# Modulation tiles beside the mixers: one PSUM bank, shifted condition columns, one turn per stage

## The chip, the cores and the metric

The kernel runs on one core of a Trainium2 chip. The metric is the device time of one execution in microseconds (us). Before the change three runs took 3722.24, 3710.8 and 3716.47 us, median 3716.47.

## The reference

Two blocks of a small transformer are computed one after the other on 256 tokens of 1024 features, both with two layers. What matters here is the modulation: a vector of conditions times a large weight matrix gives shifts, scales and gates for all tokens.

```
cond = silu(c)
for l in range(2):
    mod = cond @ w_ada[l] + b_ada[l]              # 1024 x 6144
    sh1, sc1, gt1, sh2, sc2, gt2 = split(mod, 6)
    proj = (x * (1 + sc1) + sh1) @ w_in[l]
    ... hgrn2_chunkwise and stick_breaking_attention (the mixers) ...
    ... merge, w_o, layer norm, PEER experts ...
second block, per layer i:
    mx = silu(c_2)   @ w_mod_2[i] + b_mod_2[i]    # 1024 x 9216
    mz = silu(c_ctx) @ w_mod_2[i] + b_mod_2[i]
```

## The kernel before

All large weights stream from memory in tiles of 1024 x 512 (2 MB), each as two halves of 1 MB, into `raw`, which has room for four halves. The SyncE queue issues the loads in order (`WeightStream.load`, L218); a load into a slot waits until TensorE has used the half that lay there, four halves earlier. Groups of tiles follow each other in a fixed list: `ada0`, `in0`, `beside0`, `gates0` and so on, and the first two tiles of a group are loaded while the group before it is being used. Groups with `split` are first rounded by ScalarE (`split_hi`, L263) and subtracted by VectorE (`split_lo`, L276); the modulation tiles are used as they land.

A modulation tile costs eight products. `cond` holds for each of the eight chunks of 128 features a block of 32 columns, of which the first three are the conditions and the others zero. `strip_products` (L777) multiplies chunk k into the 32 PSUM partitions from 32*(k%4), so four strips hold partial sums of the same rows. The strips are added and the row is turned into columns by four more matmuls, which take the row as the stationary operand and a 0/1 matrix `strip_sum` as the moving one.

The change is about the mixer stage of each layer (`mixers`), which is one block: all engines start it together and the next block starts when the last is through. Its own work is a chain of eight levels across the engines: VectorE makes exponents (L1301, L1303), ScalarE takes the exponential (L1265), VectorE multiplies (L1315, L1316), TensorE makes scores (L1222; L1234 at the last level), VectorE keeps them (L1288). Between these runs `StickBreaking`, one group of heads per two levels: scores (L1116), four ScalarE activations (`logs`, L1144 to L1147), VectorE (`losses`, L1157 to L1161), sums on TensorE (L1124 to L1126), VectorE (`rest`, L1166 to L1169), ScalarE (L1151), values on TensorE (L1134, L1136), and VectorE (`keep`, L1174, L1175), which the next group's scores wait for. After the levels come the outputs (L1244, L1247), their norm on VectorE (L1341 to L1351), eight transposes (L1256) and VectorE's last work (L1362, L1364), then `split_lo` for the first tile of the gates.

Beside it `SideModulation` does 12 modulation tiles in layer 0 and 10 in layer 1. `halves` puts two halves (one tile) behind each level on TensorE, and what is left behind the outputs: three tiles in layer 0, one in layer 1. Tiles alternate between two PSUM banks. `turn_row` (L1721) of tile t-1 stands between the two halves of tile t, and ScalarE's `copies` has for each tile a copy of the row out of PSUM (L1760), for which it waits until the tile's products are made, and a copy of the turned columns (L1748). A tile's first product waits until the columns two tiles back are copied. The engines execute their instructions in order, so each of these waits holds what is queued behind it. At the end VectorE adds the biases in two instructions (L1370) ahead of `split_lo`.

`input_projection` is the block ahead of the mixers. There VectorE first clears three tiles (L1031) and then waits for the first rounded weights.

## Time and profile before

| | |
|---|---|
| runs | 3722.24, 3710.8, 3716.47 us, median 3716.47 |
| span of the profiled execution | 3708.9 us (its time with what lies around it isn't listed) |
| TensorE busy | 2839.2 us, 77% |
| VectorE busy | 2476.1 us, 67% |
| ScalarE busy | 1031.3 us, 28% |
| moved by DMA | 1033.96 MB, mean 279 GB/s |
| mean granted TensorE clock | 0.878 |
| mixer stage of layer 0 | from 138.2 to 232.5 us of the span |
| mixer stage of layer 1 | from 1523.6 to 1611.2 us |

The profile is of one execution. Busy shares are means over stages with different limits. In the mixer stages all of TensorE, VectorE and ScalarE are partly idle, so which wait ends last has to be read instruction by instruction. A timeline row says when an instruction or a run of equal ones began, how long it took, and in brackets how long its engine had been idle and what ended that. An fp32 matmul has two records, so four matmuls show as x8.

### The profile page before, as it was taken

The numbers are of one execution on the slowest core, as the hardware profiler recorded it, in microseconds if no ns is written. First come the engines' busy times: TensorE is split into PE (matmuls) and PEld (weight loads), VectorE is DVE, ScalarE is ACT, GpSimd is POOL, SyncE is SP. The second block draws the span as 40 slices with busy tenths as digits, with TensorE's granted clock in tenths as the row PEclk, the third lists the DMA queues.
The fourth block names the chain that finished last, engine by engine and source line by source line (L and its number), as shares of the span: only waits on it lengthen the run. The fifth ranks groups of instructions, "written<-read, shape, count | busy, mean of one in ns | idle before, by whom it ended". The sixth has DMA issues, their size and how long they took to land. (4 is left out here: it accounts for less than half of the span.)

```text
span 3708.9 us, 42550 instructions
## 1 busy us (share of the span) xinstructions
PE 2839.2 (77%) x15748; PEld 2207.4 (60%) x15748; DVE 2476.1 (67%) x3826; ACT 1031.3 (28%) x1482; POOL 961.1 (26%) x1028
## 2 busy tenths in 40 slices
PE   6988769946399555988769920555499999999999
PEld 4677358535287215678358410111398999897797
DVE  3656876677777776646976679777655655556754
ACT  2543211010100002543110010000254454545653
POOL 0000044554544470000054557767200000000000
PEclk8999779968699877999779965868799999999999
DMA  6664799999899993554889999999555545554153
GB/s 246 212 234 153 309 390 414 413 386 374 335 389 413 372 409 126 210 200 134 352 344 414 410 358 397 408 393 409 210 186 173 171 159 171 170 185 146 62 186 127
DMA packets 225445, 1033.96 MB, mean 279 GB/s; under 512 B 29256, under 2 KB 32408, under 8 KB 167192
## 3 DMA queue, kind: packets, MB, share of 16 engines
q1 hardware_dynamic: 77848, 495.15, 36.9%
q0 software_dynamic: 147456, 536.94, 36.8%
q8 instruction: 87, 1.43, 0.2%
q14 instruction: 54, 0.44, 0.0%
HBM read 1030.94 MB, written 1.05 MB: 278 GB/s over the span
## 5 line engine op out<-in xcount | busy, mean ns | idle before, releaser
L276 DVE TENSOR_TENSOR w_lo<-raw,w_hi 128x1024 fp32r<-128x1024 f32 (+1 forms) x460 | 550.9, 1205 | 526.7 <-ACT w_hi L263 526.0
L1996 POOL DMA_INDIRECT arena_layer<-in_peer_u,arena_layer x512 | 480.5, 938 | 1360.8 <-SPq L920 959.5
L2070 DVE CUSTOM_DVE_ANT_0 arena_layer<-arena_layer,ps 128x1024 f32<-128x1024 f32 x512 | 610.9, 1219 | 172.0 <-DMA arena_layer<-in_peer_u,arena_layer 161.1
L697 PE MATMUL ps<-hT_hi,w_hi 128*128 128x256 f32 x2240 | 641.0, 286 | 41.6 <-PEq L1193 17.6
L263 ACT ACTIVATE w_hi<-raw 128x1024 fp32r<-128x1024 f32 (+1 forms) x460 | 478.6, 1044 | 668.5 <-PE ps L697 667.3
L2066 DVE SCALAR_TENSOR_TENSOR ps<-arena_layer,ps 128x1024 f32<-128x1024 f32 x428 | 551.6, 1289 | 155.2 <-DMA arena_layer<-in_peer_v,arena_layer 137.5
L697 PE MATMUL ps<-hT_lo,w_hi 128*128 128x256 f32 x2240 | 639.4, 285 | 0.0
L697 PE MATMUL ps<-hT_hi,w_lo 128*128 128x256 f32 x2240 | 639.2, 285 | 0.0
L697 PE MATMUL ps<-parts_context,raw 128*128 128x256 f32 x2496 | 548.2, 383 | 57.3 <-PEq L920 57.3
L1996 POOL DMA_INDIRECT arena_layer<-in_peer_v,arena_layer x512 | 480.4, 938 | 309.0 <-DVE ps L2066 201.8
L697 PEld LDWEIGHTS ps<-parts_context,raw 128*128 128x128 f32 x2496 | 480.0, 193 | 125.3 <-issue 58.7
L2104 PE MATMUL ps<-arena_layer,parts_context 128*128 128x512 f32 x336 | 241.1, 858 | 340.9 <-DMA arena_layer<-in_peer_v,arena_layer 219.5
L697 PEld LDWEIGHTS ps<-hT_hi,w_hi 128*128 128x128 f32 x2240 | 435.7, 195 | 44.4 <-issue 44.4
L697 PEld LDWEIGHTS ps<-hT_lo,w_hi 128*128 128x128 f32 x2240 | 435.8, 195 | 0.0
L697 PEld LDWEIGHTS ps<-hT_hi,w_lo 128*128 128x128 f32 x2240 | 435.3, 194 | 0.0
L2104 PEld LDWEIGHTS ps<-arena_layer,parts_context 128*128 128x128 f32 x336 | 79.5, 262 | 500.8 <-issue 232.6
L697 PE MATMUL ps<-raw,parts_context 128*128 128x512 f32 (+1 forms) x656 | 272.3, 578 | 12.5 <-PEq L920 12.5
L697 PE MATMUL ps<-w_hi,parts_ffn_x 128*128 128x512 f32 x704 | 221.3, 396 | 0.0
L697 PEld LDWEIGHTS ps<-raw,parts_context 128*128 128x128 f32 x656 | 126.7, 194 | 155.2 <-issue 153.0
L777 PE MATMUL ps<-raw,cond 128*32 128x512 f32 x960 | 166.3, 795 | 49.4 <-DMA raw<-in_w_mod 31.3
L697 PEld LDWEIGHTS ps<-w_hi,parts_ffn_x 128*128 128x128 f32 x704 | 132.0, 188 | 31.6
L697 PE MATMUL ps<-w_lo,parts_ffn_x 128*128 128x512 f32 x352 | 139.2, 395 | 0.0
(363 smaller groups left out, 2783.2 us busy)
## 6 DMA issues: line engine op xcount, KB each, us to landing
raw<-in_ffn_w_gu SPq DMA_DIRECT2D x154, 1024.0 KB
raw<-in_w_mod SPq DMA_DIRECT2D x72, 1024.0 KB
raw<-in_ffn_w_down SPq DMA_DIRECT2D x70, 1024.0 KB
raw<-in_w_ada SPq DMA_DIRECT2D x48, 1024.0 KB
raw<-in_w_in SPq DMA_DIRECT2D x44, 1024.0 KB
raw<-in_conv_w_in SPq DMA_DIRECT2D x24, 1024.0 KB
raw<-in_w_o SPq DMA_DIRECT2D x8, 1024.0 KB
raw<-in_w_pq SPq DMA_DIRECT2D x8, 1024.0 KB
```

The costliest lines, as they stand in the source:

```text
L263: act.activation(self.hi[:, k, 0:g.chunks(t)[k] * g.cols], self.raw_part(g, t, parity, k // 2, g.starts(t, k), g.starts(t, k + 1)), ACT.Co ...
L276: dve.tensor_tensor(self.lo[:, k, 0:n], self.raw_part(g, t, parity, k // 2, g.starts(t, k), g.starts(t, k + 1)), self.hi[:, k, 0:n].bitcas ...
L697: mm = pe.matmul(out_, stay, move, start=start and n == 0, stop=stop and n == len(combos) - 1, skip_group_check=True)
L777: mm = pe.matmul(ps[at:at + STRIP, unit, col:col + 512], cond[:, k, :], part[:, c, :], start=k < STRIPS, stop=k >= KC - STRIPS, skip_group ...
L1996: gp.indirect_dma_start(self.grow[:, slot % GR, :], None, self.tables[slot // half_way], bass.IndirectOffsetOnAxis(ap=self.index[:, k:k + ...
L2066: dve.scalar_tensor_tensor(out=self.tile, in0=row, scalar=cell, in1=self.tile, op0=ALU.mult, op1=ALU.add) \
L2070: dve.tensor_tensor_reduce(row, row, self.tile, 1.0, 0.0, ALU.mult, ALU.add, cell).then_inc(row_used.sem, 1)
L2104: mm = pe.matmul(ps[:, t, cols], self.diagonals[:, r, :], self.grow[:, k % GR, cols], start=opens and r == 0, stop=True, skip_group_check= ...
```

## The change

The tiles of a stage no longer alternate and are not turned one by one. `spread` makes a tile `wide` of 64 columns per chunk: zero, with the conditions in columns from 29 on. Tile t uses the 32 columns from 29 - conditions * t, so its rows fall on rows conditions * t and following of each strip; zeros elsewhere leave the other rows as they were, and only tile 0 opens the accumulation. All tiles add into one bank. When the last is in, ScalarE copies 128 x 512 once (`keep_rows`), TensorE turns it once against a `strip_sum` of 32 columns (`turn_rows`, behind the transposes), and VectorE adds biases straight out of PSUM, one instruction for each tile, behind `split_lo`. `spread` runs on VectorE in the input projection, behind the three clears.

```diff
-    strip_sum = sb("strip_sum", [P, 4])
+    strip_sum = sb("strip_sum", [P, STRIP])
...
-    def strip_products(pe, unit, start, part, chunks, col=0):
+    def strip_products(pe, unit, start, part, chunks, columns=cond, opens=True):
...
-            mm = pe.matmul(ps[at:at + STRIP, unit, col:col + 512], cond[:, k, :], part[:, c, :],
-                           start=k < STRIPS, stop=k >= KC - STRIPS, skip_group_check=True)
+            mm = pe.matmul(ps[at:at + STRIP, unit, 0:512], columns[:, k, :], part[:, c, :],
+                           start=opens and k < STRIPS, stop=k >= KC - STRIPS,
+                           skip_group_check=True)
...
                 for ap in cleared:
                     dve.memset(ap, 0.0)
+                beside_columns(dve, Steps(dve, vec_step))
...
                 mm.then_inc(pe_done.sem, 1)
+                beside.turn_rows(pe)
...
                     act.activation(E[:], E[:], ACT.Exp).then_inc(act_ready.sem, 1)
-                    beside.copies(act, n)
...
-                beside.copies(act, NL + 1)
                 act.wait_ge(vec_ready.sem, vec_ready.at(3 + NL))
                 act.activation(stat[:, 8:16], stat[:, 0:8], ACT.Sqrt).then_inc(act_ready.sem, 1)
-                for t in range(NL + 2, beside.tiles):
-                    beside.copies(act, t)
+                beside.keep_rows(act)
                 weights.split_hi(act, ahead)
...
-                dve.wait_ge(mod_copied.sem, mod_copied.at(beside.tiles))
-                for _, _, dst, bias in beside.targets:
-                    v.tick(dve.tensor_tensor(dst, dst, bias.unsqueeze(2).to_broadcast(dst.shape),
-                                             ALU.add))
                 weights.split_lo(dve, ahead)
+                beside.add_biases(dve, v)
...
+        HOME = STRIP - 3
...
+            self.wide = side[:, 0:2 * STRIP * KC].rearrange("p (c n) -> p c n", c=KC)
+            self.row = side[:, 2 * STRIP * KC:2 * STRIP * KC + 512]
+            self.turned = ps[:, 3, 512:512 + 4 * STRIP].rearrange("p (b n) -> p b n", n=STRIP)
...
+        def spread(self, dve, v):
+
+            v.link(dve.memset(self.wide, 0.0))
+            v.tick(dve.tensor_copy(self.wide[:, :, self.HOME:self.HOME + self.conditions],
+                                   cond[:, :, 0:self.conditions]))
 
         def halves(self, pe, first, last):
 
             for n in range(first, min(last, 2 * self.tiles)):
                 t, half = n // 2, n % 2
                 if half == 0:
-                    if t >= 2:
-
-                        pe.wait_ge(mod_copied.sem, mod_copied.at(t - 1))
...
                 start, chunks, (part,) = next(self.sections)
-                mm = strip_products(pe, 3, start, part, chunks, t % 2 * 512)
+                at = self.HOME - self.conditions * t
+                mm = strip_products(pe, 3, start, part, chunks, self.wide[:, :, at:at + STRIP], t == 0)
                 weights.section_done(mm)
-                if half == 0 and t >= 1:
-                    self.turn_row(pe, t - 1)
-                if n == 2 * self.tiles - 1:
-                    self.turn_row(pe, t)
...
+        def keep_rows(self, act):
+
+            product_wait(act, self.tiles - 1)
+            act.copy(self.row, ps[:, 3, 0:512]).then_inc(mod_rows.sem, 1)
+
+        def turn_rows(self, pe):
+
+            pe.wait_ge(mod_rows.sem, mod_rows.at(1))
+            for b in range(4):
+                mm = pe.matmul(self.turned[:, b, :], self.row[:, b * P:(b + 1) * P], strip_sum[:],
+                               start=True, stop=True)
+            mm.then_inc(mod_turned.sem, 1)
+
+        def add_biases(self, dve, v):
+
+            dve.wait_ge(mod_turned.sem, mod_turned.at(1))
+            first = 0
+            for n, kind, dst, bias in self.targets:
+                k = dst.shape[2]
+                for t in range(n):
+                    at = self.conditions * (first + t) + kind
+                    cols = slice(4 * t, 4 * t + 4)
+                    v.tick(dve.tensor_tensor(dst[:, cols, :], self.turned[:, :, at:at + k],
+                                             bias[:, cols].unsqueeze(2).to_broadcast([P, 4, k]),
+                                             ALU.add))
+                first += n
```

Three places show how the order moves. The first is TensorE at level 1 of layer 0, from the level's scores to the stick-breaking values. Before:

```order
L1222 MATMUL ps<-rows,arena_layer 128x128 x8
L777 MATMUL ps<-raw,cond 32x512 x4
L1721 MATMUL ps<-strip_sum,side_layer 128x1 x4
L777 MATMUL ps<-raw,cond 32x512 x4
L1134 MATMUL ps<-y_tok,arena_layer 64x256
L1136 MATMUL ps<-y_tok,arena_layer 64x128
```

With the change:

```order
L1127 MATMUL ps<-y_tok,tri 128x128
L1223 MATMUL ps<-rows,arena_layer 128x128 x8
L776 MATMUL ps<-raw,side_layer 32x512 x8
L1135 MATMUL ps<-y_tok,arena_layer 64x256
L1137 MATMUL ps<-y_tok,arena_layer 64x128
```

The four turning matmuls between the two halves are gone; the same holds at the other levels.

The second is ScalarE at the start of the same stage, from the first exponential to the activations of the first stick-breaking group. Before:

```order
L1265 ACTIVATE rows<-rows 128x1024
L1760 COPY side_layer<-ps 128x512
L1144 ACTIVATE arena_layer<-ps 128x768
L1145 ACTIVATE y_tok<-ps 128x768
L1146 ACTIVATE y_tok<-y_tok 128x768
```

With the change:

```order
L1267 ACTIVATE rows<-rows 128x1024
L1145 ACTIVATE arena_layer<-ps 128x768
L1146 ACTIVATE y_tok<-ps 128x768
L1147 ACTIVATE y_tok<-y_tok 128x768
L1148 ACT_TABLE_LOAD
```

No copy stands between the exponential and `logs` any more.

The third is TensorE at the end of the stage of layer 0, from the last values to the transposes. Before:

```order
L777 MATMUL ps<-raw,cond 32x512 x4
L1721 MATMUL ps<-strip_sum,side_layer 128x1 x4
L777 MATMUL ps<-raw,cond 32x512 x8
L1721 MATMUL ps<-strip_sum,side_layer 128x1 x4
L777 MATMUL ps<-raw,cond 32x512 x8
L1721 MATMUL ps<-strip_sum,side_layer 128x1 x4
L777 MATMUL ps<-raw,cond 32x512 x4
L1721 MATMUL ps<-strip_sum,side_layer 128x1 x4
L1256 MATMUL ps<-ident,y_tok 128x128 x8
```

With the change:

```order
L1135 MATMUL ps<-y_tok,arena_layer 64x256
L1137 MATMUL ps<-y_tok,arena_layer 64x128
L776 MATMUL ps<-raw,side_layer 32x512 x24
L1257 MATMUL ps<-ident,y_tok 128x128 x8
L1738 MATMUL ps<-strip_sum,side_layer 128x32 x4
```

Six halves now follow each other, and the one turn stands behind the transposes instead of four ahead of them.

## Rows read from the trace of the kernel before

**Rows 1.** Windows, both mixer stages: us, busy by engine, clock, DMA share, GB/s.

```profile
138.20:232.50 94.30, 72.75 (x568) 47.76 (x568) 64.02 (x94) 48.83 (x67) 0.00 (x0) 0.95 0.74 268
1523.60:1611.20 87.60, 66.90 (x520) 45.41 (x520) 64.06 (x94) 47.42 (x63) 0.00 (x0) 0.93 0.66 240
```

**Rows 2.** Timeline, TensorE and ScalarE, layer 0, level 0: start, us, what, idle.

```profile
140.23 0.92 PE L1116 MATMUL ps<-arena_layer 64*128 64x256 f32 x8
141.08 1.92 PE L777 MATMUL ps<-raw,cond 128*32 128x512 f32 x16
...
143.07 0.59 ACT L1760 COPY side_layer<-ps 128x512 f32<-128x512 f32 x1 [2.28 <-PE ps L777]
143.56 0.82 ACT L1144 ACTIVATE arena_layer<-ps 128x768 f32<-128x768 f32 x1
```

**Rows 3.** Timeline, one turn of two levels, layer 1, in order of time.

```profile
1545.22 0.81 ACT L1144 ACTIVATE arena_layer<-ps 128x768 f32<-128x768 f32 x1 [2.12 <-PE ps L1116]
...
1553.66 2.03 PE L1222 MATMUL ps<-rows,arena_layer 128*128 128x128 f32 x16
1555.62 1.06 PE L777 MATMUL ps<-raw,cond 128*32 128x512 f32 x8
1556.62 1.05 PE L1721 MATMUL ps<-strip_sum,side_layer 128*128 128x1 f32 x8
1557.60 1.06 PE L777 MATMUL ps<-raw,cond 128*32 128x512 f32 x8
...
1559.60 0.42 DVE L1174 CAST parts_layer<-ps 128x256 fp32r<-128x256 f32 x1 [1.23 <-PE ps L1136]
1560.53 0.92 PE L1116 MATMUL ps<-arena_layer 64*128 64x256 f32 x8 [1.06 <-DVE parts_layer L1175]
1561.50 0.81 ACT L1144 ACTIVATE arena_layer<-ps 128x768 f32<-128x768 f32 x1 [2.12 <-PE ps L1116]
```

**Rows 4.** Timeline, layer 0, behind the last level.

```profile
205.25 0.68 DVE L1337 COPY arena_layer<-ps 128x512 f32<-128x512 f32 x1
206.33 1.38 PE L1244 MATMUL ps<-arena_layer 128*128 128x128 f32 x10
```

**Rows 5.** Timeline and DMA issues (L218), layer 0, end of the stage.

```profile
210.01 1.07 PE L777 MATMUL ps<-raw,cond 128*32 128x512 f32 x8
213.12 0.35 SPq L218 DMA_DIRECT2D raw<-in_w_ada  x1
214.66 1.22 DVE L1351 TENSOR_TENSOR y_tok<-y_tok,stat 128x1024 f32<-128x1024 f32 x1
220.16 1.06 PE L777 MATMUL ps<-raw,cond 128*32 128x512 f32 x8 [0.21 <-DMA raw<-in_w_ada]
222.85 1.07 PE L1256 MATMUL ps<-ident,y_tok 128*128 128x128 f32 x8
227.35 0.28 DVE L1370 TENSOR_TENSOR adacol<-adacol,vcol 128x32 f32<-128x32 f32 x2
227.54 4.62 DVE L276 TENSOR_TENSOR w_lo<-raw,w_hi 128x1024 fp32r<-128x1024 f32 x4
```

**Rows 6.** Timeline, TensorE, layer 1, the transposes and what they waited for.

```profile
1601.44 1.10 PE L1256 MATMUL ps<-ident,y_tok 128*128 128x128 f32 x8 [0.85 <-DVE y_tok L1351]
```

**Rows 7.** The instructions on adacol, 20 to 45 us: duration ns min/median/max.

```profile
L836 DVE TENSOR_TENSOR adacol<-ps,vcol x4: 161/162/163, 24.7 to 41.3; 128x4 f32<-128x4 f32 x4
```

**Rows 8.** Timeline, VectorE, layer 0, input projection behind the clears.

```profile
61.95 1.23 DVE L276 TENSOR_TENSOR w_lo<-raw,w_hi 128x1024 fp32r<-128x1024 f32 x1 [2.66 <-ACT w_hi L263]
```

**Rows 9.** Timeline and window (columns as rows 1), falls of the clock, a longer wait.

```profile
182.70 1.22 PE L1124 MATMUL ps<-y_tok,tri 128*128 128x256 f32 x2 [1.20 <-DVE y_tok L1161]
183.00:186.00 3.00, 3.00 (x12) 2.64 (x12) 1.39 (x2) 0.58 (x3) 0.00 (x0) 0.52 0.99 355
...
1568.00:1572.00 4.00, 3.92 (x16) 3.57 (x17) 1.59 (x4) 0.95 (x3) 0.00 (x0) 0.57 0.99 371
...
150.15 0.70 PE L1124 MATMUL ps<-y_tok,tri 128*128 128x256 f32 x2 [2.19 <-DVE y_tok L1161]
```

More of the change, by code:

```diff
@@ L500, in _build @@
     mod_turned = signal("mod_turned")
-    mod_copied = signal("mod_copied")
     weights = WeightStream(raw, w_hi, w_lo, halves_landed, hi_made, lo_made, used, whole_used)
@@ L1730, in halves @@
                 if half == 0:
[L1731 to L1735 removed]
+                    self.sections = weights.sections(pe, t, t % 2, t // 2)
                 start, chunks, (part,) = next(self.sections)
[L1737 removed]
+                at = self.HOME - self.conditions * t
@@ L1751, in copies @@
-        def copies(self, act, t):
-            if t >= self.tiles:
-                return
-            product_wait(act, self.first + t)
-            if t >= 2:
-                act.wait_ge(mod_copied.sem, mod_copied.at(t - 1))
-            _, _, _, row = self.target(t)
-            act.copy(row, ps[:, 3, t % 2 * 512:(t % 2 + 1) * 512]).then_inc(mod_rows.sem, 1)
-            if t:
-                self.copy_columns(act, t - 1)
-            if t == self.tiles - 1:
-                self.copy_columns(act, t)
+        def keep_rows(self, act):
+            product_wait(act, self.tiles - 1)
+            act.copy(self.row, ps[:, 3, 0:512]).then_inc(mod_rows.sem, 1)
@@ L1770, in end_phase @@
         def end_phase(self):
-            self.first += self.tiles
-            for signal_ in (mod_rows, mod_turned, mod_copied):
-                signal_.base += self.tiles
-            if self.first == weights.group().n:
-                weights.end()
+            mod_rows.base += 1
+            mod_turned.base += 1
+            weights.end()
     def modulation_programs(l, row):
@@ L3340, in _build @@
         ke, scores, cross = work[:, 0:1024], work[:, 1024:2048], work[:, 2048:2560]
-        input_projection(l, qa, sg, km, ia, ga, qb, kb, vb, rows[:, 0, :], (rows[:, 2, :], ke, scores))
+        at = 4 * ADA_FIRST
+        own = (12 - ADA_FIRST, 0, adacol[:, l, at:48].unsqueeze(2),
+               vcol[:, 0, V_BADA + 48 * l + at:V_BADA + 48 * (l + 1)])
+        if l == 0:
+            beside = SideModulation(1, [own, (ADA_FIRST, 0, adacol[:, 1, 0:at].unsqueeze(2),
+                                              vcol[:, 0, V_BADA + 48:V_BADA + 48 + at])])
+        else:
+            beside = SideModulation(3, [own, (MOD_BESIDE, 1, modcol[:, 1, 0:4 * MOD_BESIDE],
+                                              vcol[:, 2, V_BMOD:V_BMOD + 4 * MOD_BESIDE])])
+        assert beside.tiles == BESIDE_MIXERS[l]
+        input_projection(l, qa, sg, km, ia, ga, qb, kb, vb, rows[:, 0, :], (rows[:, 2, :], ke, scores),
+                         beside.spread)
         oaT, obT = (oa_hi, oa_lo), (ob_hi, ob_lo)
```

42 lines of the change are left out of this document (6 added, 36 removed).

## The prediction

> **What bounds the kernel now.** The page's first part shows no engine full in the stages that the change touches, so I read those two stages by windows, then their timelines, engine beside engine. In them TensorE is busy 72.75 of 94.3 us and 66.90 of 87.6 us, VectorE 64 us in both, DMA moves 268 and 240 GB/s [rows 1]; the reader is to see that neither is full, so what counts is the chain of waits between engines. The rest of the kernel is not touched. It starts each block when the block before ends and its weights run at most two tiles ahead, so a stage that ends earlier moves all that follows by the same amount, and I carry the savings to the end at full size.
>
> The chain can be followed over two levels, after which it repeats [rows 3]. ScalarE starts the logarithms at 1545.22 and the next turn's at 1561.50: 16.28 us. Between lie its activations and the next exponential, VectorE's two products, the level's scores on TensorE (1553.66), a half tile (1555.62), the turning of the tile before (1556.62), a half tile (1557.60), the values, VectorE's `keep` (1559.60) and the next scores (1560.53). At `keep` VectorE had been idle for 1.23 us, waiting for TensorE; ScalarE at 1561.50 for 2.12 us, also for TensorE. So at levels 1, 3 and 5 what stands in TensorE's queue ahead of the values is on the path. At even levels it is not: behind the two halves TensorE waits 1.20 us for VectorE [rows 9].
>
> At level 0 another wait ends last. The first stick-breaking scores start at 140.23, but L1144, which reads them, starts at 143.56: ahead of it in ScalarE's queue stands the copy L1760, idle 2.28 us until both halves of tile 0 are done [rows 2]. At the end of layer 0's stage the normed output is ready at 215.88 (214.66 + 1.22), yet its transposes start at 222.85 because TensorE still has side tiles to do [rows 5]. In layer 1, where only one tile is left there, the transposes wait for VectorE instead [rows 6].
>
> **The change part by part.**
>
> Level 0. With the copy gone L1144 can start 0.97 us after the scores, the distance from 1560.53 to 1561.50 in rows 3: at 141.20 instead of 143.56. Saving 2.36 us; the same pattern stands in layer 1, once per layer.
>
> Turns at levels 1, 3, 5. From 1556.62 to 1557.60 is 0.98 us [rows 3]. VectorE's 1.23 us of idle time covers it, so nothing of VectorE takes its place: 3 x 0.98 = 2.94 us per layer. The turns at even levels and their copies cost nothing today and save nothing; there TensorE's wait only grows from 1.20 to about 2.2 us.
>
> Turn at the last level. L1244 starts at 206.33, when TensorE comes free, but needs VectorE's L1337, done at 205.93 [rows 4]. With 0.07 us for the signal, as from TensorE's end at 143.00 to the copy at 143.07 [rows 2], it can start at 206.00: 0.33 us, not 0.98. VectorE is late next.
>
> So the outputs begin 2.36 + 2.94 + 0.33 = **5.63 us** earlier in each layer.
>
> The tail of layer 0. The six halves behind the values now follow each other, with neither turns nor waits for copied columns. The second of them frees the slot of the last, which makes it the step to follow. Before it began at 210.01 + 1.00 (a half) + 0.98 (the turn) = 211.99, the load was issued 1.13 us later at 213.12, and 7.04 us after that, at 220.16, the first product that waited for it ran [rows 5]. Now the first half starts at 210.01 - 5.63 = 204.38, the second at 205.38, the issue is at 206.51, and with the same 7.04 us the last half runs at 213.55. It takes 1.0 us, then the transposes start at 214.55 instead of 222.85: **8.3 us**, of which 5.63 are those above. So DMA is late next, not the norm (ready at 210.25). The landing could be 1 us sooner, or 2 later since four loads are now issued 1 us apart.
>
> The tail of layer 1. VectorE's chain sets it [rows 6], so it gets the 5.63 us and nothing more.
>
> Biases. Today two additions of 0.28 us together stand ahead of `split_lo`, from 227.35 to 227.54: 0.19 us of path [rows 5]. Now 12 and 10 additions out of PSUM stand behind it, where nothing covers them, since the block ends with VectorE. One of this form took 162 ns alone [rows 7]; the pair in rows 5 started some 0.1 us apart. Bounds 0.1 and 0.162 us each; I take 0.1, as nothing here waits between them. 2.2 us added, 0.4 removed: **1.8 us** lost.
>
> Edits at nothing. The spread (a clear of 512 columns and a small copy, under 1.2 us) runs where VectorE idles 2.66 us before its first split [rows 8]; without that cover it would cost its own length. The one row copy and turn per stage lie under VectorE's products and the split, some 9 us. `strip_sum` has 32 columns instead of 4, in a load among many at the start. The order of the weight loads is unchanged. The products keep their shape and number; the second half of a tile accumulates already today, at 1.06 us like the first [rows 3], so adding into one bank costs nothing.
>
> The clock. In these stages it fell twice to its lower level, 1.2 GHz: 0.52 granted from 183 to 186 us, 0.57 from 1568 to 1572 [rows 9]. TensorE worked throughout; half of 3 us is lost, 1.5 us a fall. Both came where TensorE had done a half, a turn, a half and then waited 1.20 us at an even level; six other such waits had no fall. The waits grow to 2.2 us at levels 2, 4 and 6. Against more falls speaks the wait at level 0, 2.19 us today without a fall (the same in layer 1) [rows 9]. The turns, with one moving column, may already have counted as little work. I take three falls in both stages in place of two: 1.5 us lost.
>
> The Trainium skill's page "TensorE: Matmul & The Clock Gate", section "HAM oscillation — how this bites in real kernels", says that waits between bursts of matmuls take the clock back to half, to be paid at each burst. That speaks against a change that turns TensorE work into waiting; rows 9 agree in two of eight cases and disagree in the rest.
>
> Sum against the profiled execution: 8.3 (layer 0) + 5.63 (layer 1) - 1.8 - 1.5 = **10.6 us** less, a span of 3698.3. That execution's own time isn't listed; the median of the runs, 3716.47, is 7.6 above its span, so I forecast 3716.5 - 10.6 = **3705.9 us**, or 0.29% less. About 0.3%, 11.15 us, is what a measurement can tell from no change.
>
> **The rivals.**
>
> *The clock hardly falls.* If 1.20 and 2.2 us are both harmless and two falls were chance, none remain: 12.1 (the sum without the clock) + 3.0 = 15.1 us, 3701.4. With one fall 13.6.
>
> *The clock falls at most long waits.* Five or six falls, three or four more than today: 12.1 - 3 or 4 times 1.5 = 6 to 8 us, 3709 to 3710; with the dear end of the additions (another 1.2 us) 3711.5.
>
> *DMA takes the tail.* Four loads in flight delay the last beside half in layer 0 by 2 to 3 us. The rate there reaches 371 GB/s in busy stretches [rows 9], some 2.8 us for a half. Then 8 us, 3708.5.
>
> *Slower.* The clock falls at every level, the odd ones too, where TensorE's waits come closer together once the turn between them is gone. Each fall costs 1.5 us; 16 levels in both stages less the two falls of today leave 14, so up to 21 us against 12.1: 3718 to 3725. It decides from the ninth additional fall. Against it stand six waits of eight without one.
>
> *The copy is not what held the logarithms at level 0.* Then 2.36 us per layer stay: 10.6 - 4.7 = 5.9 us, 3710.6. Against it: at 1561.50, with no copy between, L1144 starts 0.97 us after the scores [rows 3], and at level 0 it starts within the copy's 0.59 us [rows 2].
>
> **How the numbers follow.** My forecast 0.45, few falls 0.22, many falls 0.17, DMA 0.11, the copy innocent 0.02, slower 0.03. The forecast's own spread (landing, additions, run to run) puts some two fifths of it beyond 11.15 us. Faster: 0.22 + 0.19 + 0.02 = 0.43. Slower by over 0.3%: 0.02, as even most of that rival stays inside. Same: 0.55. The low end is no fall and an early landing, 3701.4 less 1 and some noise: 3699.5; the high end many falls with dear additions and a late landing, 3713.
>
> **What would show it.** No L1721 rows between halves; L1144's counterpart starting near 141.2; a turn of two levels of 15.3 us; L1244's counterpart near 200.7; in layer 0 the last half starting near 213.5 and waiting for DMA, the block ending near 224.9 instead of 232.2; in layer 1 the stage 87.6 - 4.8 = 82.8 us long without a change of its falls; 12 and 10 additions at 0.1 us behind the split. Wrong would be a turn still at 16.3 us, additions of 0.16 us or more, granted clocks near 0.5 in several stretches of the stages, or a saving that is there at 233 us and gone by the end of the span.

## The result and the profile after

The changed kernel took 3673.01 us, median of 4 runs (3666.79 to 3686.11), against 3717.41 (3710.80 to 3722.24) of the kernel before: a ratio of 0.9888 with a 95% interval of 0.9872 to 0.9904. That is 44.4 us less where I had forecast 10.6, and below my range. All times and ratios here leave out disturbed runs, of which there were three, all of the kernel before in the second batch below (4283 to 7639 us). The profiled execution took 3674.26 us with a span of 3672.5, so 36.4 us less span than the one before.

The same two windows as in [rows 1], for the changed kernel (us, busy by engine, clock, DMA share, GB/s):

```profile
142.94:231.14 88.20, 63.59 (x480) 40.29 (x481) 64.68 (x104) 42.16 (x44) 0.00 (x0) 0.91 0.75 286
...
1504.41:1585.76 81.35, 57.17 (x448) 38.20 (x449) 64.55 (x102) 41.94 (x44) 0.00 (x0) 0.92 0.69 259
```

From its first instruction to the next block's first product a stage lasted 94.47 us (138.23 to 232.70) and 87.71 us (1523.61 to 1611.32) before. The stages are 94.47 - 88.20 = 6.3 us and 87.71 - 81.35 = 6.4 us shorter. TensorE lost 9 to 10 us of work in each, VectorE none. So some 12.6 us of the 36.4 lie where the change lies. To find the rest I took equal instructions of both traces and followed how far apart they start. The first difference is some 4.5 us the wrong way, there already at 41 us of the span, ahead of the input projections, where the first loads landed later. It isn't the change's: two later traces of the kernel before with nothing but padding (`b_shift96`, `b_arena96`) begin their mixers 3.2 and 3.8 us later than it as well. Two stretches that the diff does not touch then bring 26 us. They begin 126 and 101 us behind the mixer stages, with the first split tile of the experts' queries, and end with the first split tile behind the experts. The last 1044 us are equal. Before:

```profile
358.40:1447.30 1088.90, 765.13 (x3099) 527.21 (x3098) 801.67 (x1346) 125.44 (x233) 480.63 (x512) 0.83 0.92 365
1712.60:2664.70 952.10, 554.36 (x1987) 321.87 (x1985) 726.07 (x1267) 106.04 (x222) 480.29 (x512) 0.78 0.92 362
```

With the change:

```profile
354.30:1428.10 1073.80, 764.26 (x3112) 526.01 (x3111) 800.40 (x1348) 126.47 (x233) 479.67 (x512) 0.83 0.92 370
1687.00:2628.40 941.40, 559.09 (x1987) 322.66 (x1985) 723.27 (x1266) 105.95 (x222) 479.62 (x512) 0.76 0.91 366
```

Every engine does the same work there to within 1% at nearly the same clock (0.83 in both; 0.78 and 0.76), yet the stretches are 15.1 and 10.7 us shorter, at 370 instead of 365 GB/s. DMA's share is 0.92 or 0.91 in all of them: these stages hang on the DMA. The fifth part of the profile's page says which transfers. Before:

```profile
L2070 DVE CUSTOM_DVE_ANT_0 arena_layer<-arena_layer,ps 128x1024 f32<-128x1024 f32 x512 | 610.9, 1219 | 172.0 <-DMA arena_layer<-in_peer_u,arena_layer 161.1
...
L2066 DVE SCALAR_TENSOR_TENSOR ps<-arena_layer,ps 128x1024 f32<-128x1024 f32 x428 | 551.6, 1289 | 155.2 <-DMA arena_layer<-in_peer_v,arena_layer 137.5
```

With the change (the same lines, now 12 lower):

```profile
L2058 DVE CUSTOM_DVE_ANT_0 arena_layer<-arena_layer,ps 128x1024 f32<-128x1024 f32 x512 | 607.5, 1219 | 148.2 <-DMA arena_layer<-in_peer_u,arena_layer 142.3
...
L2054 DVE SCALAR_TENSOR_TENSOR ps<-arena_layer,ps 128x1024 f32<-128x1024 f32 x428 | 551.8, 1289 | 136.9 <-DMA arena_layer<-in_peer_v,arena_layer 119.0
```

Each instruction takes 1219 and 1289 ns in both; VectorE's idle time ahead of them, for the gathers of the peer tables, fell from 172.0 + 155.2 to 148.2 + 136.9 us, 42.1 less. The DMA queue of the gathers itself, on the page of before and of after:

```profile
q0 software_dynamic: 147456, 536.94, 36.8%
```

```profile
q0 software_dynamic: 147456, 536.94, 36.5%
```

The same packets and bytes took 0.368 x 3708.9 = 1365 us of each engine before and 0.365 x 3672.5 = 1340 after, 1.8% less. What had changed for a gather into the arena? Its address. The tiles' sizes sum up to their addresses if each is rounded up to 32 bytes: `strip_sum` with 4 columns took 32 bytes of each partition, with 32 columns it takes 128. All tiles allocated behind it, `arena` and `parts` among them, moved by 96 bytes. In the built programs the arena began at byte 153248 of the partition before, 160 past a multiple of 256, and begins at 153344 now, a multiple of 256. The eight slots into which rows are gathered begin 10752 bytes, 42 times 256, behind the arena's start and are 4096 bytes apart, so they share its distance from a multiple of 256.

### The profile page after: what moved, and what is told of

Its sections match the earlier page's. It is cut to its first block and busy times, and to the rows that moved or that the text cites. A ratio compares the mean times of both kernels' runs of the same rounds, so it can differ in the third digit from the quotient of the medians.

```text
span 3672.5 us, 42174 instructions
## 1 busy us (share of the span) xinstructions
PE 2827.0 (77%) x15588; PEld 2197.2 (60%) x15588; DVE 2473.9 (67%) x3848; ACT 1018.5 (28%) x1440; POOL 959.5 (26%) x1028
## 5 line engine op out<-in xcount | busy, mean ns | idle before, releaser
L2058 DVE CUSTOM_DVE_ANT_0 arena_layer<-arena_layer,ps 128x1024 f32<-128x1024 f32 x512 | 607.5, 1219 | 148.2 <-DMA arena_layer<-in_peer_u,arena_layer 142.3
L263 ACT ACTIVATE w_hi<-raw 128x1024 fp32r<-128x1024 f32 (+1 forms) x460 | 478.5, 1044 | 669.0 <-PE ps L696 667.4
L2054 DVE SCALAR_TENSOR_TENSOR ps<-arena_layer,ps 128x1024 f32<-128x1024 f32 x428 | 551.8, 1289 | 136.9 <-DMA arena_layer<-in_peer_v,arena_layer 119.0
L776 PE MATMUL ps<-raw,cond 128*32 128x512 f32 x608 | 121.0, 917 | 47.1 <-DMA raw<-in_w_mod 29.1
```

The source lines that it names most:

```text
L263: act.activation(self.hi[:, k, 0:g.chunks(t)[k] * g.cols], self.raw_part(g, t, parity, k // 2, g.starts(t, k), g.starts(t, k + 1)), ACT.Co ...
L776: mm = pe.matmul(ps[at:at + STRIP, unit, 0:512], columns[:, k, :], part[:, c, :], start=opens and k < STRIPS, stop=k >= KC - STRIPS, skip_ ...
L2054: dve.scalar_tensor_tensor(out=self.tile, in0=row, scalar=cell, in1=self.tile, op0=ALU.mult, op1=ALU.add) \
L2058: dve.tensor_tensor_reduce(row, row, self.tile, 1.0, 0.0, ALU.mult, ALU.add, cell).then_inc(row_used.sem, 1)
```

## The experiments

They had to separate the scheduling of the mixer stages from this shift. They ran in four batches, each on one chip, and each ratio is to the kernel before in the same batch (medians there 3718.13, 3826.31, 3719.04 and 3719.27 us). The record numbers the chips 12, 3, 11 and 3, and doesn't say whether the second and fourth batch had the same one. In the second batch every kernel was 3% slower, before included.

### First batch: the shift without the edits, and the edits without the shift

The kernel before, its later tiles moved by 96 bytes (`b_shift96`):

```diff
     ln_eps = sb("ln_eps", [P, 1])
+    shift = sb("shift", [P, 24])
     rows = sb("rows", [P, 3, D])
```

> The kernel before with an unused tile of 96 bytes per partition ahead of rows, nothing else: rows, context_kT, context_v, the arena and the parts lie where they lie with the change (the arena at byte 153344, a multiple of 256, instead of 153248, which is 160 past one). Theory A (addresses): the two expert stages, 27.8 us shorter in the trace after than in the one before, are shorter because rows landing in the arena no longer straddle a boundary; expected 25 to 32 us faster than before, some 3689 us, 4 KB packets of the gathers at 159 ns instead of 161 in the middle. Theory B (the edits to the side tiles do all of it, by what they leave of instructions and by where the later stages fall): no change, 3717 us within 5.

Measured: 3688.85 us, 0.992 (0.9906 to 0.9934), so 29.3 us faster by an unused tile alone.

The change with 160 bytes more (`a_shift160`; the arena is then 160 past a multiple of 256, as before), and with 64 (`a_shift64`):

```diff
     ln_eps = sb("ln_eps", [P, 1])
+    shift = sb("shift", [P, 40])
     rows = sb("rows", [P, 3, D])
```

```diff
+    shift = sb("shift", [P, 16])
```

> The change with an unused tile of 160 bytes ahead of rows, so that the arena is again 160 past a multiple of 256, as before. Theory A: the edits alone are left, 12 to 16 us faster than before (3701 to 3705 us), both mixer stages as short as with the change. Theory B: as the change, 43 us faster, 3673 us.

> The change with an unused tile of 64 bytes ahead of rows: the arena is 64 past a multiple of 256 but on a multiple of 64. Theory A in two forms: if a multiple of 64 (or 32) bytes is enough, as the change, 3673 us; if only a multiple of 256 is, as slow as with 160 bytes, 3700 us or so. Theory B: 3673 us.

Measured: 3703.99 us, 0.9964 (0.995 to 0.9977), for the first, 14.1 us faster than before; 3697.16 us, 0.9937 (0.9915 to 0.9959), for the second. With the arena put back the expert stretches of `a_shift160` are those of the kernel before:

```profile
356.80:1448.80 1092.00, 770.47 (x3115) 530.18 (x3114) 802.61 (x1348) 126.43 (x233) 479.58 (x512) 0.83 0.92 364
1707.70:2659.70 952.00, 555.86 (x1987) 321.69 (x1985) 725.09 (x1266) 105.95 (x222) 479.57 (x512) 0.78 0.92 362
```

So the two parts add up: 29.3 + 14.1 = 43.4 us, against 44.4 for the change, which was measured apart from this batch. The edits alone are worth 14.1 us, 9 to 19 by the interval. That is the number that my 10.6 stood for, and lies in my range (3704 against 3699.5 to 3713). Other pairs give the same or more: 14.7 us in the third batch (50.8 for the change less 36.1 for the address alone), 19.2 in the fourth (`a_shift128_b`), and 21.0 by `a_shift64`, whose runs lie 23 us apart. A saving of 19 or 21 us would lie beyond my range, so it proves little that 14.1 lies within it.

The change with `raw`, into which all weights are loaded, on a multiple of 256 as well (it lies 128 past one in both kernels). Three small tiles go ahead of it (`a_raw256`):

```diff
+    scol = sb("scol", [P, KC])
+    bcol = sb("bcol", [P, KC])
+    lbcol = sb("lbcol", [P, DEPTH, 2, HG_HEADS])
     raw = sb("raw", [P, 4, 2 * QUARTER])
...
-    scol = sb("scol", [P, KC])
-    bcol = sb("bcol", [P, KC])
-    lbcol = sb("lbcol", [P, DEPTH, 2, HG_HEADS])
```

> The change with scol, bcol and lbcol (128 bytes) allocated ahead of raw: raw lies on a multiple of 256 (16640) instead of 128 past one (16512); the arena stays. If only multiples of 256 are good for landing weights, the weight loads (8 KB packets, 309 ns in the middle) get shorter by up to 1 or 2%, and the DMA-bound expert stages with them, 5 to 15 us faster than the change. If 64 is enough, as the change, 3673 us. Theory B: as the change.

Measured: 3667.49 us, 0.9863 (0.9847 to 0.988). That is 5.5 us under the change, which wasn't in this batch; whether `raw` does it was open, and repeated below.

### Second batch: the single terms

The wait at level 0 put back without the copy (`a_wait0`):

```diff
                     act.activation(E[:], E[:], ACT.Exp).then_inc(act_ready.sem, 1)
+                    if n == 0:
+                        product_wait(act, 0)
```

> The change with one wait put back: at level 0 ScalarE waits for the products of tile 0 ahead of the logarithms, as the copy L1760 made it do; no copy. Theory (the copy's wait is what held level 0): L1145 starts 2.4 us later against the scores, the distance from the first to the second run of the level's scores is 9.07 us again instead of 6.7, in both layers, 4.7 us slower than the change. Rival (level 0 is held by something else as well, or the time is made up before the block ends): the distance stays 6.7 us, or the block ends as early, 0 us.

ScalarE and TensorE at level 0, of the changed kernel:

```profile
144.94 0.92 PE L1117 MATMUL ps<-arena_layer 64*128 64x256 f32 x8
...
145.91 0.81 ACT L1145 ACTIVATE arena_layer<-ps 128x768 f32<-128x768 f32 x1 [0.41 <-PE ps L1117]
```

and of `a_wait0`:

```profile
142.29 0.92 PE L1117 MATMUL ps<-arena_layer 64*128 64x256 f32 x8
...
145.13 0.81 ACT L1145 ACTIVATE arena_layer<-ps 128x768 f32<-128x768 f32 x1 [2.28 <-PE ps L776]
```

The logarithms start 0.97 us behind the scores in the one, exactly the distance that I had taken, and 2.84 us in the other. So the wait alone costs 1.87 us a layer; the copy's own 0.5 us made up the rest of 2.36. The next level's scores follow 8.59 instead of 6.71 us later, not 9.07 as I had expected, since the copy isn't there. By time it was 3787.36 us, 0.9909 (0.9884 to 0.9934), which with an interval of 19 us cannot show a term of 4.

The turns put back as four one-column products between the halves, with nothing that waits for them (`a_turns`):

```diff
                 weights.section_done(mm)
+                if half == 0 and t >= 1 or n == 2 * self.tiles - 1:
+                    for b in range(4):
+                        pe.matmul(self.turned[:, b, 0:1], ident[:], strip_sum[:, 0:1],
+                                  start=True, stop=True)
```

> The change with four matmuls of one moving column put back between the halves of every tile (out of ident, so that they wait for nothing), and behind the last; nothing reads them. Theory (a turn ahead of the values is on the path): a turn of two levels takes 16.1 to 16.3 us instead of 15.15, the last level 0.3 us more, 6.5 to 7.5 us slower than the change in both layers together; the tail of layer 0 hides its three turns behind DMA. Rival (VectorE takes the place of the turn): no more than 2 us. As to the clock: if turns count as little work, the falls stay as many as in the change; if they are work enough, fewer.

Measured: 3800.39 us, 0.9935 (0.9917 to 0.9953), 13.0 us slower than `a_wait0` and 17.9 slower than `a_raw160` below. The times of this batch can't carry a term of 7 us: the runs of `a_wait0` lie at 3785 to 3789 and at 3805 to 3807 us, and of the 17.9 us some 15 lie in the expert stretches of the traces (2136.2 against 2120.8 us), where `a_turns` changes nothing. The trace of the levels is plainer. TensorE of `a_turns`, layer 0, one even level:

```profile
174.65 2.05 PE L1223 MATMUL ps<-rows,arena_layer 128*128 128x128 f32 x16 [0.40 <-DVE arena_layer L1315]
176.63 1.06 PE L776 MATMUL ps<-raw,side_layer 128*32 128x512 f32 x8
177.62 1.05 PE L1730 MATMUL ps<-strip_sum,ident 128*128 128x1 f32 x8
178.60 1.07 PE L776 MATMUL ps<-raw,side_layer 128*32 128x512 f32 x8
180.87 0.70 PE L1125 MATMUL ps<-y_tok,tri 128*128 128x256 f32 x2 [1.20 <-DVE y_tok L1162]
182.73 1.48 PE L1223 MATMUL ps<-rows,arena_layer 128*128 128x128 f32 x11
```

The level lasts 182.73 - 174.65 = 8.08 us with the turn, as it does without: the turn eats a wait here. Odd levels last 8.1 to 8.2 us with it and 7.08 without. That makes 3 x 1.1 x 2 = 6.7 us in both layers, and a turn of two levels of 16.2 to 16.3 us, as expected. Both mixer stages together are 177.7 us in this trace, against 171.1 and 173.7 in the two of its batch that have the change's stages (`a_shift128`, `a_raw160`), which have more falls of the clock. The tail didn't hide all of its turns: 15.15 us from the outputs to the transposes in layer 0, against 14.1 to 14.5. In layer 0 the clock never fell in the levels (66.28 us at 1.00), only behind them; in layer 1 it fell once, just ahead of the last level:

```profile
138.72:205.00 66.28, 58.25 (x465) 39.59 (x466) 48.78 (x71) 37.46 (x38) 0.00 (x0) 1.00 0.76 267
205.00:229.58 24.58, 15.49 (x114) 9.98 (x113) 15.93 (x33) 4.80 (x6) 0.00 (x0) 0.75 0.78 306
...
1630.50:1634.00 3.50, 3.50 (x13) 3.14 (x14) 2.59 (x3) 0.30 (x1) 0.00 (x0) 0.51 0.97 372
```

The change with 128 bytes more (`a_shift128`), to tell whether a multiple of 128 is enough, and with `scol` alone ahead of `raw`, which puts `raw` 160 past a multiple of 256 and leaves the arena (`a_raw160`):

```diff
+    shift = sb("shift", [P, 32])
```

```diff
+    scol = sb("scol", [P, KC])
     raw = sb("raw", [P, 4, 2 * QUARTER])
...
-    scol = sb("scol", [P, KC])
```

> The change with an unused tile of 128 bytes ahead of rows: the arena is 128 past a multiple of 256. If a boundary every 128 bytes is what a landing row must start on, as the change, 3673 us, 4 KB packets at 159 ns throughout; if 256 bytes, as with 64 and 160 bytes, 3697 to 3704 us, packets of 161 ns in the middle and 169 at the slow end.

> The change with scol alone allocated ahead of raw: raw, and all up to adacol, lie 32 bytes further on, 160 past a multiple of 256; rows, the arena and the parts stay on one. Theory A: the packets of the weights (8 KB, half the bytes moved) get longer as those of the gathers did, so that the page's time of queue q1 grows; the expert stages, which DMA bounds, slow by 5 to 15 us, and the stages bound by TensorE do not: 3678 to 3688 us. Rival (only the gathers mind, since theirs are the rows that one packet fills): 3673 us.

Measured: 3803.98 us, 0.9945 (0.9926 to 0.9964), and 3782.51 us, 0.9887 (0.9864 to 0.9911). The second has the ratio that the change had at first, so my expectation that `raw` would cost 5 to 15 us at 160 isn't borne out, though the interval of 18 us leaves room for its low end. The first is undecided here: five of its runs lie at 3802 to 3808 us and two at 3780 and 3782. One of these two was profiled, and its expert stretches, 2129.5 us, lie among those of the three kernels of this batch with the arena on a multiple of 256 (2120.8 to 2139.3 us). So I ran it again.

### Third batch: the change again, the arena alone, and TensorE's waits filled

The change unaltered (`a_again`), and the kernel before with the 96 bytes behind `context_v`, so that only `arena` and `parts` move (`b_arena96`):

```diff
     context_v = sb("context_v", [P, TT, NKV * HD])
+    shift = sb("shift", [P, 24])
     ps = ctx.enter_context(nc.psum_tensor("ps", [P, 4, 1024], F32))
```

> The change itself, unaltered, beside the other three on their chip. Expected the same ratio to before as on the first chip, 0.9888; on the chip of a_wait0 and a_turns, where the kernel before took 3829 us, it hasn't been run. If the ratio holds here, those two are read against 0.9888.

> The kernel before with the 96 unused bytes behind context_v, so that the arena and the parts alone move onto a multiple of 256; rows, context_kT and context_v stay 160 past one. Theory (the gathers mind where they land, and they land in the arena): as b_shift96, a ratio of 0.992. Rival (what TensorE and VectorE read from rows and the context tiles matters): a good part of the 29 us stays away.

Measured: 3668.24 us, 0.9858 (0.9841 to 0.9874), and 3682.93 us, 0.9899 (0.9883 to 0.9916), 36.1 us faster than before. So none of the tiles between `strip_sum` and the arena is needed for it. `parts` moves too, but in these stretches no transfer goes there. The change itself came to 50.8 us here, against 44.4 when it was first measured: the same kernel's ratio differs by 0.003, some 11 us, from batch to batch, and differences across batches are to be read with that in mind. The expert stretches of `b_arena96`, to be read against the rows of before and after above:

```profile
363.00:1440.00 1077.00, 761.45 (x3112) 525.02 (x3111) 800.69 (x1347) 126.45 (x233) 480.96 (x512) 0.83 0.92 369
1706.80:2644.70 937.90, 554.79 (x1987) 318.46 (x1985) 724.90 (x1266) 106.04 (x222) 480.76 (x512) 0.77 0.92 368
```

The change with three halves instead of two at levels 2, 4 and 6 (`a_fill3`), and with four (`a_fill4`). The halves are those that would otherwise stand in the tail:

```diff
-                    beside.halves(pe, 2 + 2 * n, 4 + 2 * n)
+                    beside.some(pe, 3 if n in (2, 4, 6) else 2)
...
+        def some(self, pe, count):
+            self.halves(pe, self.done, self.done + count)
+            self.done = min(self.done + count, 2 * self.tiles)
```

```diff
-                    beside.some(pe, 3 if n in (2, 4, 6) else 2)
+                    beside.some(pe, 4 if n in (2, 4, 6) else 2)
```

> The change, and at levels 2, 4 and 6 three halves in place of two in TensorE's 2.3 us of waiting; three (layer 0) or none (layer 1) are left behind the outputs in place of six and two. Theory: the wait hides the third half, and in layer 0 the transposes come when DMA has brought three halves fewer behind the outputs: 4 us earlier, up to the norm. With TensorE less idle the clock falls less often, 1.5 us for each fall. Together 4 to 8 us faster than the change. Rival: the halves aren't there in time and TensorE, waiting for DMA, holds the sums: as the change or slower.

> As a_fill3 with four halves at levels 2, 4 and 6: all 24 are done before the outputs. Two halves take 1.93 us of the 2.3. DMA must bring six halves in a turn of 15.15 us, 415 GB/s, about what it reached in this stage at its end (421). Theory: 5 to 10 us faster than the change if it keeps up. Rival: it does not, TensorE waits for halves ahead of the sums at levels 4 and 6, and layer 0's levels get longer by what the tail saves.

Measured: 3664.55 us, 0.9854 (0.9838 to 0.987), and 3668.62 us, 0.9861 (0.9845 to 0.9877); by time neither can be told from `a_again`, so the 4 to 8 and 5 to 10 us that I expected aren't shown. In the trace of `a_fill3` layer 0's stage is 80.7 us instead of 87.7: no fall in its levels, and hardly a tail. TensorE's wait at an even level is shorter, and the level lasts 8.08 us as before:

```profile
174.44 2.05 PE L1223 MATMUL ps<-rows,arena_layer 128*128 128x128 f32 x16 [0.40 <-DVE arena_layer L1315]
176.42 2.78 PE L776 MATMUL ps<-raw,side_layer 128*32 128x512 f32 x24
180.67 0.70 PE L1125 MATMUL ps<-y_tok,tri 128*128 128x256 f32 x2 [1.46 <-DVE y_tok L1162]
```

Up to the outputs the clock stays at its higher level in both layers:

```profile
140.79:201.40 60.61, 50.16 (x409) 31.48 (x409) 48.77 (x71) 35.98 (x37) 0.00 (x0) 1.00 0.85 326
1496.45:1557.05 60.60, 49.28 (x400) 31.32 (x401) 48.73 (x71) 35.96 (x37) 0.00 (x0) 1.00 0.85 327
```

With four halves it is too much, as the rival had it: steps of 9.3 us appear in layer 0's levels at full clock, and the stages last 85.9 and 83.7 us.

### Fourth batch: the boundary, `raw` again, and the best version

The change (`a_third`), the change with 128 bytes more (`a_shift128_b`), the change with `raw` aligned (`a_raw256_b`), and `a_fill3` with `raw` aligned (`best_fill3`); their edits stand above.

> The change itself again, beside the other three. A ratio of 0.986 to 0.989, as twice before.

> a_shift128 again, now beside the change. Its packets of 4 KB had 172 ns at the slow end on the other chip, so 256 bytes are the boundary: 24 to 30 us slower than a_third, like 64 and 160 bytes. If 128 is enough: as a_third.

> a_raw256 again, now beside the change. The 8 KB packets were at 309 ns with raw at 128 and at 160 past a multiple of 256 as well as on one, so raw's address costs nothing: within 3 us of a_third. If it does cost: 5 us faster again.

> The change with raw on a multiple of 256 and three halves at levels 2, 4 and 6 (a_fill3). In a_fill3's trace the two stages took 162.2 us against 173.0 in a_again's. Expected 4 to 10 us faster than a_third, and faster than both kernels of this case.

Measured: `a_third` 3667.44 us, 0.9862 (0.9842 to 0.9881). `a_shift128_b` 3700.12 us, 0.9954 (0.9936 to 0.9971), 32.7 us slower than `a_third`: 128 past a multiple of 256 is as bad as 160 or 64, and costs a little more than the 24 to 30 us that I expected. `a_raw256_b` 3665.58 us, 0.9868 (0.9849 to 0.9886), not to be told from `a_third`. `best_fill3` 3655.93 us, 0.9842 (0.9823 to 0.986), 11.5 us faster than `a_third` by the medians, though the intervals of the two ratios overlap. It has the lowest median of all versions and clearly beats the kernel before; that it beats the change is likely but not shown by time. Its stages, 162.3 against 169.8 us in the traces, speak for it. The stretches, first of `a_third`, then of `a_shift128_b`:

```profile
353.60:1425.40 1071.80, 759.25 (x3099) 519.98 (x3098) 800.62 (x1349) 125.40 (x232) 479.65 (x512) 0.83 0.92 371
1684.30:2623.90 939.60, 557.42 (x1987) 320.86 (x1985) 722.83 (x1267) 105.94 (x222) 479.60 (x512) 0.76 0.91 367
```

```profile
352.90:1445.00 1092.10, 766.48 (x3115) 528.12 (x3115) 802.96 (x1349) 126.46 (x233) 479.53 (x512) 0.83 0.92 364
1704.00:2661.50 957.50, 571.72 (x1987) 324.94 (x1985) 726.44 (x1266) 105.95 (x222) 479.51 (x512) 0.74 0.92 360
```

In `best_fill3` hardly a tail is left in layer 0: the transposes wait for VectorE's norm, and DMA holds back only one half, by 0.60 us.

```profile
205.94 1.07 PE L776 MATMUL ps<-raw,side_layer 128*32 128x512 f32 x8 [0.60 <-DMA raw<-in_w_ada]
209.35 1.09 PE L1257 MATMUL ps<-ident,y_tok 128*128 128x128 f32 x8 [2.34 <-DVE y_tok L1350]
```

All kernels with the stages of before or of the change, but those of the second batch, together, with what the gathers' single packets (4 KB each) took by the records of the traces, and the two expert stretches summed:

```
arena past a multiple of 256   packet, ns (5, 50, 95%)   stretches, us
160: before, a_shift160        159 / 161 / 169           2040.9, 2044.1
 64: a_shift64                 159 / 161 / 169           2053.5
128: a_shift128_b              159 / 160 / 172           2049.6
  0: the change, three runs    159 / 159 / 159           2015.2, 2012.9, 2011.4
  0: b_shift96, b_arena96      159 / 159 / 159           2014.4, 2014.9
  0: a_raw256, a_raw256_b      159 / 159 / 159           2016.7, 2015.4
```

Nothing lies between 2017 and 2040. The packets are a little longer and, above all, no longer even. Outside the second batch their mean is 165.4 to 165.6 ns at 64, 128 and 160 past and 162.0 to 162.4 on a multiple, so the distance itself doesn't matter.

The same records show what the weights' packets (8 KB each, into `raw`) do in these stretches. While the gathers run (from the first to the last issue in a stretch) and the arena is on a multiple of 256, they take 309 ns, with at most 0.6% at 310 to 330, whether `raw` lies 0, 128 or 160 past one. With the arena off a multiple, 68 to 81% of them take 310 to 330 ns, 314 or 315 in the middle, though `raw` lies where the change has it. So gathers into an unaligned arena lengthen their neighbours' packets as well as their own. Where no gathers run, the address of `raw` shows: 13 to 35% of the packets take 310 to 330 ns with `raw` 128 or 160 past a multiple, and 1% in `a_raw256`, `a_raw256_b` and `best_fill3`. For `a_raw160` I had expected longer packets, and later took 309 ns in the middle for no effect. There is one, of some 10 ns in a part of the packets, and too small for the times to show.

## Why the prediction was wrong

**The step that failed** is the last of the edits at nothing: "`strip_sum` has 32 columns instead of 4, in a load among many at the start", with the sentence "The rest of the kernel is not touched" ahead of it. I counted the load and not the room. `a_shift160` and `b_shift96` show that 29 of 44 us hang on it, and `b_arena96` that it is the arena. Of the four distances that were run, 0, 64, 128 and 160 past a multiple of 256, only 0 is fast. The Trainium skill's page "DMA: Bandwidth & Descriptors", section "How a descriptor splits into AXI transactions", says that a transaction must start at a multiple of 256 bytes, so that for a descriptor which doesn't start there the bytes below its start are fetched unused and still cost. It speaks of reads, and what moved here is where the gathers write. The boundary of 256 agrees: 64, 128 and 160 past are slow alike, 2041 to 2054 us against 2011 to 2017. That the cost would grow with the unused bytes doesn't: the gathers' packets have the same mean at all three.

With the address set aside the sum was near, 10.6 against 12.6 us in this pair of traces, and its terms can be read there one by one.

**Level 0** was right: 2.36 forecast, and the distance from level 0's scores to the next ones fell from 9.07 to 6.71.

**Turns** were slightly too cheap. From [rows 3] a turn of two levels lasted 16.28 us; now, in layer 0, 176.59 - 161.43 = 15.16:

```profile
161.43 2.05 PE L1223 MATMUL ps<-rows,arena_layer 128*128 128x128 f32 x16 [0.40 <-DVE arena_layer L1315]
163.41 1.92 PE L776 MATMUL ps<-raw,side_layer 128*32 128x512 f32 x16
167.65 0.70 PE L1125 MATMUL ps<-y_tok,tri 128*128 128x256 f32 x2 [2.32 <-DVE y_tok L1162]
...
169.51 2.03 PE L1223 MATMUL ps<-rows,arena_layer 128*128 128x128 f32 x16
...
176.59 2.05 PE L1223 MATMUL ps<-rows,arena_layer 128*128 128x128 f32 x16 [0.40 <-DVE arena_layer L1315]
```

1.12 us less, not 0.98. The turn's start to the next half's start was not all of its price: in `a_turns` the values begin 2.98 us after an odd level's first half, and in `a_fill3`, whose odd levels have two halves in one row, 1.86 us. The wait at even levels grew from 1.20 to 2.32, forecast 2.2. The last level cannot be read from this trace, since a fall of the clock lies across it. In layer 0 of `a_again`, where none does, the outputs start 3.70 us behind the last level's scores and wait for VectorE, as forecast; before it was 206.33 - 202.29 (L1234) = 4.04 us, so 0.34 for my 0.33:

```profile
198.59 1.14 PE L1235 MATMUL ps<-rows,arena_layer 128*128 128x128 f32 x8
...
202.29 1.38 PE L1245 MATMUL ps<-arena_layer 128*128 128x128 f32 x10 [0.71 <-DVE arena_layer L1336]
```

**The tail of layer 0** went as forecast, DMA late next. Its rows, to be read against [rows 5]:

```profile
209.51 2.78 PE L776 MATMUL ps<-raw,side_layer 128*32 128x512 f32 x24
212.70 1.07 PE L776 MATMUL ps<-raw,side_layer 128*32 128x512 f32 x8 [0.41 <-DMA raw<-in_w_ada]
215.60 1.06 PE L776 MATMUL ps<-raw,side_layer 128*32 128x512 f32 x8 [1.83 <-DMA raw<-in_w_ada]
218.08 1.93 PE L776 MATMUL ps<-raw,side_layer 128*32 128x512 f32 x8 [1.42 <-DMA raw<-in_w_ada]
219.95 1.77 PE L1257 MATMUL ps<-ident,y_tok 128*128 128x128 f32 x8
```

The stage began 4.71 us later in this trace, so the last half ran at 218.08 - 4.71 = 213.4, forecast 213.55. Two differences cancel in that: the load was issued at 206.8 (211.50 in the trace) for my 206.51, and its product ran 6.6 us behind it instead of 7.04. It took 1.93 us and not 1.06, at the lower clock, and the transposes 1.77 instead of 1.07. They began at 215.2 where I had 214.55.

**Biases** were too dear: 12 in 0.91 us and 8 in 0.63, under 0.08 each, forecast 0.1; in layer 1 they stand as a row of 8 and one of 2. Each lasts some 150 ns, but they start 69 ns apart. With the two old additions gone from ahead of the split, both stages lost 1.1 us in all instead of 1.8.

```profile
225.15 4.63 DVE L276 TENSOR_TENSOR w_lo<-raw,w_hi 128x1024 fp32r<-128x1024 f32 x4
229.70 0.91 DVE L1751 TENSOR_TENSOR adacol<-ps,vcol 128x4 f32<-128x4 f32 x12
...
1584.45 0.63 DVE L1751 TENSOR_TENSOR adacol<-ps,vcol 128x4 f32<-128x4 f32 x8
1585.00 0.22 DVE L1751 TENSOR_TENSOR modcol<-ps,vcol 128x8 f32<-128x8 f32 x2
```

**The clock** fell three times in the levels of this trace, as forecast, before twice, and once more in the tail. In layer 0 at 184 and 201, around waits of 2.3 us, and at 218; in layer 1 once at 1559:

```profile
182.00:188.00 6.00, 5.18 (x28) 4.94 (x28) 4.27 (x8) 1.46 (x3) 0.00 (x0) 0.72 0.73 303
198.00:203.00 5.00, 3.46 (x18) 3.32 (x19) 4.44 (x7) 1.87 (x2) 0.00 (x0) 0.79 0.96 388
210.00:222.00 12.00, 8.34 (x61) 3.06 (x53) 6.21 (x10) 2.12 (x4) 0.00 (x0) 0.86 1.00 407
...
1558.00:1563.00 5.00, 3.56 (x13) 3.20 (x14) 3.91 (x6) 1.76 (x2) 0.00 (x0) 0.66 0.95 390
```

That three came is partly luck, for the reason wasn't borne out. In the prediction I counted eight waits of 1.20 us before, two with a fall; there are three a layer, so six, and four without a fall. The kernel before with padding alone had four falls in its levels (`b_shift96`) and three (`b_arena96`), so that kernel's profiled execution with two had few: with turns and waits of 1.2 us it is three in the mean of three traces. The ten traces with the levels of the change, waits of 2.3 us, have two to five, 3.2 in the mean. So the longer waits are not shown to add falls. `a_turns`, with one, speaks against my guess that turns count as little work, but one trace against the three of the kernel before settles nothing. A fall cost what I took: it lies over two levels, 8.88 + 7.85 us here instead of 15.16, so 1.6 us; at the last level some 0.7. The fall in the tail cost 0.9 us in the last half and 0.7 in the transposes.

Together, in this pair of traces: level 0 and the last level as forecast; the turns saved 0.8 us more than forecast, the tail, its fall of the clock included, 0.3 less; biases cost 0.7 less, and the clock outside that tail 0.8 less. That makes 12.6 instead of 10.6. Over all traces the two stages sum to 182.2, 189.6 and 186.3 us with the old order (mean 186.0) and, without the second batch, to 169.5 to 173.0 in eight with the new one (mean 170.6), 15.4 us apart, which fits the 14 to 15 us by time of the first and third batch. With more traces I'd have taken a kernel before with three falls.

**The rivals.** That DMA would hold the tail by another 2 to 3 us did not happen; the copy was not innocent; and the clock didn't fall at every level. "Faster" had 0.43 (two fifths of 0.45 are 0.18, so its terms give 0.42), and that was too low, for it had no case in it by which untouched stages change.

What stays open: why 64, 128 and 160 bytes past cost the same; by what way the gathers lengthen the weights' packets too; and why the second batch took 3% longer. In that batch nearly all the time lies in the expert stretches, 1125.6 and 995.2 us in `a_raw160`, with a tail behind them of 1045 us as against 1044. Its gathers' packets are at 159 ns up to the 95% point, but their 99% point is at 389 to 411 ns where the arena is on a multiple of 256, against 211 to 236 in the other batches.

## What to carry to other kernels

When a tile's size changes, compare the addresses of all tiles behind it: here 96 bytes decided over 29 us, some twice what the edits did, and an unused tile of 96 bytes gets them alone. Before a saving is ascribed to an edit, run the kernel before with the new addresses and the change with the old ones. Where an engine waits in a loop and has a tail of the same work behind it, move as much of the tail into the waits as fits them, and no more.

## What the runs showed of the hardware

- The start of a gather's target in SBUF, by its distance from a multiple of 256 bytes, changes 4 KB packets from 159 ns (5% to 95% point) to 159 to 172; 64, 128 and 160 bytes past are alike. In stages whose DMA share is 0.92 that costs 29 to 36 us of 3700.
- While such gathers run, the 8 KB packets of weight loads lengthen too, from 309 to 314 or 315 ns in the middle, at an unchanged address of their own.
- With waits of 2.3 us in the even levels every one of 20 stages, in ten traces, had one to three falls of the clock in its levels. With a third half of side work in them (waits of 1.46 us) none of four stages had one (`a_fill3`, `best_fill3`: 1.00 from the start to the outputs).
- A fall inside the levels costs 1.5 to 1.6 us, spread over two levels: 16.6 to 16.7 us instead of 15.16.
- The granted clock can be low in a tail that waits for DMA: 1.93 us for a half that takes 1.06.
- Additions out of PSUM of 128 x 4, some 150 ns long, start 69 ns apart when they stand in a row.
